# High and low rows side by side: matmuls of 256, 288 and 272 columns in place of three of 272

## The chip, the cores and the metric

The kernel runs on one core of a Trainium2 chip. The time is that of the device for one execution, in microseconds; lower is better.

## The reference

One decoder block on 256 tokens with 16 learned meta tokens ahead of them (272 rows in all), width 2048, all in float32. `hs` is the residual stream:

```
hs = concat([meta, x])                                     # (272, 2048)
hs = hs + 0.5 * swiglu(rmsnorm(hs, g1), gate1, up1, down1) # width 5632 inside
u  = rmsnorm(hs, gm) @ w_in + b_in                         # 5 groups of 1024: b, c, v, a, g
y_sc = b * causal_dwconv(c * v, 3 taps)
y_cf = silu(layernorm(causal_dwconv(a * sigmoid(g), 31 taps) + bias))
hs = hs + concat([y_sc, y_cf]) @ w_out
hs = hs + 0.5 * swiglu(rmsnorm(hs, g2), gate2, up2, down2)
out = rmsnorm(hs, gf)[16:]                                 # meta rows dropped
```

## The kernel before

The core holds everything transposed: 128 channels in the partitions, tokens along the free axis, so a tile of the residual stream is 128 x 272 and there are 16 of them (`res`). A weight block of 512 KB (`raw`) is fetched from HBM by SP, in a ring of 4. ScalarE rounds it to float32r as its high half (`high`, L726), VectorE subtracts and writes the low half (`low`, L955), TensorE takes both. Activations are kept as such halves as well: `x_hi` and `x_lo` (written by `operand`, ScalarE L734 and VectorE L964), and `a_hi` and `a_lo` for the hidden layer of the FFN (L777, L1039). `product` (L522 to L528) then does a tile of output as three matmuls into one PSUM bank: high weight with high activation, high weight with low, low weight with high. Each has its own weight load of 128 x 128.

The stages in order, with the groups of output columns, the blocks of a group and the columns of a matmul: gu1 (gate and up of the first FFN; 22 groups of 8 blocks, 272), down1 (4 of 22, 272), ag (4 of 8, 272), cv (4 of 8, 260: the 256 tokens and four meta tokens that the short convolution looks back on), b (2 of 8, 256), out_sc and out_cf (4 of 4 each, 256), gu2 (22 of 8, 256), down2 (4 of 22, 512, with tokens in the partitions). A block is 24 matmuls, in down2 12. A group of results fills 4 of the 8 PSUM banks, and the next group the other 4.

Each engine's program runs in its written order. VectorE empties a group's banks during the third block of the next group (`finish` at step 0, L1026 and L1028, times `rstd`), and the rest of the group's work stands at the next two blocks. ScalarE's share stands after its fourth to sixth weight block. In ag, cv, b and out_sc both engines also do the 31-tap convolution (`conv_products`, `conv_adds`), a fixed number of taps after each block (`spread`).

Addresses are chosen by hand, modulo 256 bytes. A row of `x_hi` or `a_hi` is 272 elements, 1088 bytes, so that the starts of successive rows move on by 64: 192, 0, 64, 128. gu1, down1, ag and b take the rows of a block from one such class (`down_rows`, `b_rows`, every fourth row) and write the weight block at the address 64 bytes past the class (`w_class`, `w_same`, `w_kept`). gu2 and the out stages have rows of 1024 bytes at class 192 and weights at class 0. cv takes rows in order, with weights at class 0 throughout.

Of the kernel before, what the change touches and what calls it, by code (L numbers as in the profile page):

```python
# [26 lines left out]
ALU = mybir.AluOpType  # L27
# [4 lines left out]
P = 128  # L32
# [7 lines left out]
def build(nc, x, meta_tokens, ffn1_norm, ffn1_w_gate, ffn1_w_up, ffn1_w_down, mix_norm, w_in, b_in,  # L40
# [40 lines left out]
    with ExitStack() as ctx:  # L81
# [9 lines left out]
        ROW_BLOCK, BUFFER = T, 4 * T  # L91
        sb("to_rows", [P, (192 - nc.sbuf_base) % 256 // 32 * 8])
# [4 lines left out]
        gain1 = sb("gain1", [P, KD])  # L97
# [3 lines left out]
        assert w_at % 256 == 0 and x_at % 256 == a_at % 256 == 192 and 4 * BUFFER % 256 == 0  # L101
# [21 lines left out]
        x_hi = at("x_hi", x_at, [P, KD, T], F32R)  # L123
        x_lo = at("x_lo", x_at + 4 * KD * T, [P, KD, T], F32R)
        x2_hi = at("x2_hi", x_at + 0, [P, KD, SEQ], F32R)
        x2_lo = at("x2_lo", x_at + 0 + 4 * KD * SEQ, [P, KD, SEQ], F32R)

        def weights(name, rows, pitch, shift):

            n = BLOCK // rows  # L130
            lead = shift(0) % 32 // 4
            both = [[at(f"{name}_{part}{s}", w_at + 4 * (BUFFER * (RING * b + s) - lead) + shift(s),
                        [P, rows, pitch], F32R)[:, :, lead:lead + n] for s in range(RING)]
                    for b, part in enumerate(("hi", "lo"))]
            assert all(shift(s) + 4 * ((rows - 1) * pitch + n) <= 4 * BUFFER for s in range(RING))
            return both

        NEAR = SEQ + -(-(SCW - 1) // 4) * 4
        w_rows = weights("w_rows", 4, ROW_BLOCK, lambda s: 0)
        w_class = [weights(f"w_class{q}_", 4, 256, lambda s: 256 // 4 * q) for q in range(4)]  # L140
        w_same = [weights(f"w_same{q}_", 2, BANK, lambda s: 256 // 4 * q) for q in range(4)]
        w_kept = [weights(f"w_kept{q}_", 2, BANK, lambda s: 256 // 4 * q + 4 * META) for q in range(4)]
        w_next = {q: weights(f"w_next{q}_", 2, BANK + META, lambda s: 256 // 4 * q) for q in (0, 2)}


        down_rows = []
        for q in (0, 2):
            up, down = list(range(q, KF, 4)), list(range(q + 1, KF, 4))[::-1]
            turn_at = up + down
            down_rows += [tuple(sorted(turn_at[t:t + 2])) for t in range(0, len(turn_at), 2)]  # L150
        assert sorted(k for pair in down_rows for k in pair) == list(range(KF))
        assert all(b - a in (1, 4) for a, b in down_rows)

        b_rows = [(k, k + 4) for q in range(4) for k in (q, q + 8)]
        assert len(b_rows) == N_B

        def block_weights(phase, g, i):

            s = slot(phase, g, i)
            if phase in ("gu1", "ag"):  # L160
                both = w_rows if isinstance(g, int) and g == 0 else w_class[i // 2]
            elif phase == "down1":
                a, b = down_rows[i]
                both = w_same[a % 4] if b == a + 4 else w_next[a % 4]
            elif phase == "b":
                both = w_kept[b_rows[i][0] % 4]
            else:
                both = w_class[0] if phase in ("cv", "gu2") else w_same[0]
            return both[0][s], both[1][s]

        def raw_rows(phase, s):
# [5 lines left out]
        a1_hi = at("a_hi", a_at, [P, KF, T], F32R)  # L177
        a1_lo = at("a_lo", a_at + 4 * KF * T, [P, KF, T], F32R)
        a2_both = at("a2_both", a_at + 64, [P, 2, KF, SEQ], F32R)
        a_of = {"gu1": (a1_hi, a1_lo),  # L180
                "gu2": (a2_both[:, 0, :, :], a2_both[:, 1, :, :])}
# [7 lines left out]
        mix_at = a_at + 0  # L189
# [28 lines left out]
        def param(name, i):  # L218
            if name == "ffn1":
                return gain1[:, i:i + 1]  # L220
            return par[:, 0, row0[name] + i:row0[name] + i + 1]

# [49 lines left out]
        ident_doubled = sem("ident_doubled")  # L272
        res_turned, res_copied, res_added = sem("res_turned"), sem("res_copied"), sem("res_added")
# [62 lines left out]


# [29 lines left out]
        def _(sp):  # L367
# [27 lines left out]
            def paired(phase, wa, wb, col_a, col_b):  # L395

                rows = [w.rearrange("(q c p) n -> q p c n", c=4, p=P) for w in (wa, wb)]
                every_fourth = [w.rearrange("(c q p) n -> q p c n", q=4, p=P) for w in (wa, wb)]

                def body(g, parity):  # L400
                    for i in range(n_blocks[phase]):
                        if phase == "gu1" and isinstance(g, int) and g == 0:
                            for q in {0: (0,), 2: (1,), 4: (2, 3)}.get(i, ()):
                                load_x(q)
                        apart = phase in ("gu1", "ag") and not (isinstance(g, int) and g == 0)
                        src = (every_fourth if apart else rows)[i % 2][
                            i // 2, :, :, bass.ds(g * 256 + (col_a, col_b)[i % 2], 256)]
# [70 lines left out]
        def _(pe):  # L478
# [43 lines left out]

            def product(bank, n, w_high, w_low, act_high, act_low, first, last):
# [26 lines left out]
            def paired(phase, norm):  # L550
                toks = tokens(phase)

                def body(g, parity):
# [6 lines left out]
                    for i in range(n_blocks[phase]):  # L560
# [8 lines left out]
                        for j, c in ([(j, c) for j in range(2) for c in range(4)] if phase in ("cv", "gu2")  # L569
                                     else [(j, c) for c in range(4) for j in range(2)]):  # L570
                                k = i // 2 + 4 * c if phase in ("gu1", "ag") and not first_group else 4 * (i // 2) + c
                                if norm and first_group and i % 2 == 0 and j == 0:
                                    pe.wait_ge(xlo_ready[norm], k + 1)
                                if opening and i == 0 and c == 2 and j == 0:
# [3 lines left out]
                                moving = ((x2_hi[:, k, :], x2_lo[:, k, :]) if phase == "gu2"  # L578
                                          else (x_hi[:, k, toks], x_lo[:, k, toks]))
                                m = product(bank, width[phase], w_hi[:, c, cols], w_lo[:, c, cols],  # L580
                                            *moving, k == 0, k == KD - 1)
# [7 lines left out]
            def pairs_group(phase, g, row_pairs, high, low):  # L589

                toks = tokens(phase)
                start_group(phase, g)
                for i, rows in enumerate(row_pairs):
                    start_block(phase, g, i)
                    if phase == "down1" and g == 0:
                        pe.wait_ge(alo_ready["gu1"], max(max(pair) for pair in down_rows[:i + 1]) // 2 + 1)
                    w_hi, w_lo = block_weights(phase, g, i)
                    for c, k in enumerate(rows):
                        for j in range(SET):
                            cols = slice(j * P, (j + 1) * P)  # L600
                            m = product(SET * (g % 2) + j, width[phase], w_hi[:, c, cols], w_lo[:, c, cols],
                                        high[:, k, toks], low[:, k, toks], i == 0 and c == 0,
                                        i == len(row_pairs) - 1 and c == 1)
# [22 lines left out]
            def last_group(g):  # L626
# [7 lines left out]
                def half_block(i, h):  # L634
# [3 lines left out]
                        for c in range(2):  # L638
                            k = 2 * i + c
                            w_high, w_low = (w[:, c, :] for w in block_weights("down2", g, i))  # L640
                            a_hi, a_lo = a_of["gu2"]
                            pe.matmul(dst, a_hi[:, k, toks], w_high, start=k == 0, stop=False)  # L642
                            pe.matmul(dst, a_lo[:, k, toks], w_high, start=False, stop=False)  # L643
                            m = pe.matmul(dst, a_hi[:, k, toks], w_low, start=False, stop=k == KF - 1)  # L644
# [53 lines left out]
            for g in range(G_D):  # L698
                pairs_group("down1", g, down_rows, a1_hi, a1_lo)
            paired("ag", "down1")  # L700
            paired("cv", None)
            for g in range(G_B):
                pairs_group("b", g, b_rows, x_hi, x_lo)
# [13 lines left out]
        def _(act):  # L717
# [10 lines left out]
            def operand(phase, norm, t):  # L728
# [4 lines left out]
                dst = x2_hi[:, t, :] if phase == "gu2" else x_hi[:, t, toks]  # L733
                act.activation(dst, res[:, t, toks], ACT.Copy,  # L734
# [619 lines left out]
```

## Time and profile before

| what | us |
|---|---|
| median of 3 runs | 1851.77 |
| lowest, highest of them | 1849.19, 1852.44 |
| span of the profiled execution (no other total is listed for it) | 1847.9 |
| TensorE, VectorE, ScalarE busy in that span | 1836.8, 1089.4, 902.2 |

The span reaches from the first to the last instruction of that execution. Matmuls are pipelined: a new one starts before the last has ended, so their busy time is not the sum of their durations, and their spacing has to be read from windows or starting times.

### The profile page before, as it was taken

The numbers are of one execution on the slowest core, as the hardware profiler recorded it, in microseconds if no ns is written. First come the engines' busy times: TensorE is split into PE (matmuls) and PEld (weight loads), VectorE is DVE, ScalarE is ACT, GpSimd is POOL, SyncE is SP. The second block draws the span as 40 slices with busy tenths as digits, with TensorE's granted clock in tenths as the row PEclk, the third lists the DMA queues.
The fourth block names the chain that finished last, engine by engine and source line by source line (L and its number), as shares of the span: only waits on it lengthen the run. The fifth ranks groups of instructions, "written<-read, shape, count | busy, mean of one in ns | idle before, by whom it ended". The sixth has DMA issues, their size and how long they took to land.

```text
span 1847.9 us, 34890 instructions
## 1 busy us (share of the span) xinstructions
PE 1836.8 (99%) x14421; PEld 1792.6 (97%) x14421; DVE 1089.4 (59%) x1230; ACT 902.2 (49%) x1151; POOL 5.8 (0%) x16
## 2 busy tenths in 40 slices
PE   9999999999999999999999999999999999999998
PEld 9999999999999999999999999999999999988886
DVE  7555555555554555369899887555555555544454
ACT  6434334344443444359888665444444444444443
POOL 1000000000000000000000000000000000000000
PEclk9999999999999999999999999999999999999999
DMA  7655555555567777755666566666666666666664
GB/s 229 193 177 178 174 181 174 178 178 174 181 172 180 177 177 179 179 175 175 185 184 180 176 209 192 194 194 192 193 192 194 192 194 192 215 193 189 193 189 135
DMA packets 283359, 342.29 MB, mean 185 GB/s; under 512 B 10639, under 2 KB 223985, under 8 KB 283152
## 3 DMA queue, kind: packets, MB, share of 16 engines
q1 hardware_dynamic: 282672, 340.44, 61.7%
q8 instruction: 59, 0.97, 0.2%
q10 hardware_dynamic: 320, 0.53, 0.1%
q0 software_dynamic: 288, 0.19, 0.0%
q14 instruction: 20, 0.16, 0.0%
HBM read 339.02 MB, written 2.10 MB: 185 GB/s over the span
## 4 chain that ended last, share of the span: by engine, by line
PE 97%; ACT 1%; DVE 1%; DMA 1%; issue 0%; SPq 0%; DVEq 0%
PE ps L526 28%; PE ps L528 28%; PE ps L527 28%; PE ps L642 4%; PE ps L643 4%; PE ps L644 4%; ACT tap_product L833 0%; DMA raw<-in_w_out 0%; DMA m_rows<-in_meta_tokens 0%; PE ps L660 0%; PE ps L488 0%; DVE w_same__lo L955 0%; ACT w_same__hi L726 0%; ACT y_f L850 0%; PE ps L667 0%
## 5 line engine op out<-in xcount | busy, mean ns | idle before, releaser
L528 PE MATMUL ps<-x_hi,w_class__lo 128*128 128x272 f32 (+2 forms) x3200 | 901.6, 282 | 0.0
L526 PE MATMUL ps<-x_hi,w_class__hi 128*128 128x272 f32 (+2 forms) x3200 | 900.8, 281 | 0.1
L527 PE MATMUL ps<-x_lo,w_class__hi 128*128 128x272 f32 (+2 forms) x3200 | 900.3, 281 | 0.0
L955 DVE TENSOR_TENSOR w_class__lo<-raw,w_class__hi 128x1024 fp32r<-128x1024 f32 x400 | 489.3, 1224 | 421.1 <-ACT w_class__hi L726 419.7
L726 ACT ACTIVATE w_class__hi<-raw 128x1024 fp32r<-128x1024 f32 x400 | 424.3, 1061 | 564.1 <-PE ps L528 563.8
L527 PEld LDWEIGHTS ps<-x_lo,w_class__hi 128*128 128x128 f32 x3200 | 602.3, 188 | 0.0
L526 PEld LDWEIGHTS ps<-x_hi,w_class__hi 128*128 128x128 f32 x3200 | 601.5, 188 | 0.3 <-PE ps L542 0.3
L528 PEld LDWEIGHTS ps<-x_hi,w_class__lo 128*128 128x128 f32 x3200 | 601.6, 188 | 0.0
L955 DVE TENSOR_TENSOR w_same__lo<-raw,w_same__hi 128x1024 fp32r<-128x1024 f32 x200 | 244.1, 1224 | 256.9 <-ACT w_same__hi L726 256.7
L726 ACT ACTIVATE w_same__hi<-raw 128x1024 fp32r<-128x1024 f32 x200 | 211.5, 1060 | 315.7 <-PE ps L528 170.6
L528 PE MATMUL ps<-a_hi,w_same__lo 128*128 128x272 f32 x640 | 183.4, 287 | 0.0
L526 PE MATMUL ps<-a_hi,w_same__hi 128*128 128x272 f32 x640 | 183.4, 287 | 0.0
L527 PE MATMUL ps<-a_lo,w_same__hi 128*128 128x272 f32 x640 | 183.3, 286 | 0.0
L642 PE MATMUL ps<-w_same__hi,a_both 128*128 128x512 f32 x352 | 137.3, 390 | 0.0
L644 PE MATMUL ps<-w_same__lo,a_both 128*128 128x512 f32 x352 | 137.0, 389 | 0.0
L643 PE MATMUL ps<-w_same__hi,a_both 128*128 128x512 f32 x352 | 137.0, 389 | 0.0
L527 PEld LDWEIGHTS ps<-a_lo,w_same__hi 128*128 128x128 f32 x640 | 120.6, 188 | 0.0
L526 PEld LDWEIGHTS ps<-a_hi,w_same__hi 128*128 128x128 f32 x640 | 120.5, 188 | 0.0
L528 PEld LDWEIGHTS ps<-a_hi,w_same__lo 128*128 128x128 f32 x640 | 120.5, 188 | 0.0
L833 ACT ACTIVATE tap_product<-z,par 128x256 f32<-128x256 f32 x232 | 98.8, 495 | 0.0
L644 PEld LDWEIGHTS ps<-w_same__lo,a_both 128*128 128x128 f32 x352 | 66.1, 188 | 13.8
L642 PEld LDWEIGHTS ps<-w_same__hi,a_both 128*128 128x128 f32 x352 | 66.1, 188 | 13.6
(170 smaller groups left out, 1509.5 us busy)
## 6 DMA issues: line engine op xcount, KB each, us to landing
raw<-in_ffn_w_up SPq DMA_DIRECT2D x176, 512.0 KB, 3.5
raw<-in_ffn_w_down SPq DMA_DIRECT2D x176, 512.0 KB, 4.9
raw<-in_ffn_w_gate SPq DMA_DIRECT2D x175, 512.0 KB, 3.5
raw<-in_w_in SPq DMA_DIRECT2D x80, 512.0 KB, 3.6
raw<-in_w_out SPq DMA_DIRECT2D x32, 512.0 KB, 4.8
x_tok<-in_x SPq DMA_DIRECT2D x4, 512.0 KB, 8.4
gain_tok<-in_final_norm SPq DMA_DIRECT2D x1, 1024.0 KB, 4.6
out_y<-o_tok SPq DMA_DIRECT2D x2, 512.0 KB, 2.8
```

The costliest lines, as they stand in the source:

```text
L526: pe.matmul(dst, w_high, act_high, start=first, stop=False)
L527: pe.matmul(dst, w_high, act_low, start=False, stop=False)
L528: return pe.matmul(dst, w_low, act_high, start=False, stop=last)
L642: pe.matmul(dst, a_hi[:, k, toks], w_high, start=k == 0, stop=False)
L643: pe.matmul(dst, a_lo[:, k, toks], w_high, start=False, stop=False)
L644: m = pe.matmul(dst, a_hi[:, k, toks], w_low, start=False, stop=k == KF - 1)
L726: act.activation(block_weights(phase, g, i)[0], raw_rows(phase, s), ACT.Copy).then_inc(hi_ready, 1)
L833: act.activation(tap_product[:, q % PRODUCTS, c % 2, :], z[:, c, 2 + n:2 + n + SEQ], ACT.Copy, scale=cf_tap(2 + n, c)).then_inc(cf_product, 1)
L955: dve.tensor_tensor(w_lo, raw_rows(phase, s), w_hi.bitcast(F32), ALU.subtract).then_inc(lo_ready, 1)
```

## The change

A row of moving data now holds one tile's high and low part side by side: high of the 256 tokens, high of the 16 meta tokens, low of the 16 meta tokens, low of the 256 tokens, 544 elements or 2176 bytes. Row starts are at 0 or 128 modulo 256 bytes. The middle of a row is read in one piece by the product of the high weight with the low part, which takes the high meta part along; the first matmul needs only the 256 tokens. The meta results come out in two pieces of the bank, which VectorE adds. In gu1, down1 and ag the three matmuls have 256, 288 and 272 columns, in cv 256, 276 and 272. b reads the same rows with three of 256. `in_rows` (`e` below) is 16, in cv 4; `in_order` is true in the first group of gu1 and ag alone; `add_meta_pieces` is one tensor_reduce from two pieces of 4 banks to 4 x e columns in SBUF.

```
+        HIGH_SEQ, HIGH_META = slice(0, SEQ), slice(SEQ, T)
+        LOW_META, LOW_SEQ = slice(T, T + META), slice(T + META, 2 * T)
...
+            def product_of_rows(phase, bank, w_high, w_low, row, first, last):
+                e = in_rows[phase]
+                seq = slice(e + META, e + META + SEQ)
+                pe.matmul(ps[:, bank, seq], w_high, row[:, HIGH_SEQ], start=first, stop=False, skip_group_check=True)
+                pe.matmul(ps[:, bank, 0:seq.stop], w_high, row[:, T - e:2 * T], start=False, stop=False,
+                          skip_group_check=True)
+                return pe.matmul(ps[:, bank, seq.start:seq.stop + META], w_low, row[:, 0:T], start=False, stop=last,
+                                 skip_group_check=True)
```

Weights and rows: there are two classes instead of four, 0 and 128, with the weights 64 bytes on; in the first group of gu1 and ag the weights stay at 64. cv takes every second row too.

```
+        w_class = [weights(f"w_class{q}_", 4, 256, 64 + 128 * q) for q in range(2)]
+        w_pair = [weights(f"w_pair{q}_", 2, BANK, 64 + 128 * q) for q in range(2)]
+        w_kept = [weights(f"w_kept{q}_", 2, BANK, 64 + 128 * q, 64 + 128 * (1 - q)) for q in range(2)]
+        def two_apart(n):
+            return [(k, k + 2) for first in range(0, n, 4) for k in (first, first + 1)]
+        down_rows, b_rows = two_apart(KF), two_apart(KD)
...
+            if in_order(phase, g):
+                return 4 * (i // 2) + c
+            q = i // 2
+            return 8 * (q // 2) + q % 2 + 2 * c
```

VectorE, in `finish` (gu1, ag, cv at step 0; down1 has the reduce and one addition into `res` instead):

```
+                        if phase in in_rows:
+                            add_meta_pieces(phase, bank)
...
+                            dve.tensor_tensor(piece, piece, over_two(rstd[:, toks.start:toks.start + e], e, SET),
+                                              ALU.mult).then_inc(meta_scaled[phase], 1)
+                            dve.wait_ge(meta_scaled[phase], g + 1)
+                            dve.wait_ge(emptied, read + 4)
+                            dve.tensor_tensor(t12[:, :, 0:e], t12[:, :, 0:e], piece,
+                                              ALU.add).then_inc(meta_whole[phase], 1)
```

ScalarE's SiLU, sigmoid and Identity at that place now wait for `meta_whole` instead of `emptied`. `operand` and the halves of `a` are written in two instructions each on ScalarE and VectorE, one for the tokens and one for the meta tokens:

```
-                dst = x2_hi[:, t, :] if phase == "gu2" else x_hi[:, t, toks]
-                act.activation(dst, res[:, t, toks], ACT.Copy,
+                    act.activation(x_rows[:, t, HIGH_SEQ], res[:, t, META:T], ACT.Copy,
...
+                    act.activation(x_rows[:, t, HIGH_META], res[:, t, 0:META], ACT.Copy,
```

gu2, out_sc, out_cf and down2 keep their lengths and their addresses modulo 256.

## Rows read from the trace of the kernel before

**Rows 1.** The page: the span, and busy time, share, instructions of each engine.
```profile
span 1847.9 us, 34890 instructions
...
PE 1836.8 (99%) x14421; PEld 1792.6 (97%) x14421; DVE 1089.4 (59%) x1230; ACT 902.2 (49%) x1151; POOL 5.8 (0%) x16
```

**Rows 2.** The page: the chain that ended last, shares of the span by engine.
```profile
PE 97%; ACT 1%; DVE 1%; DMA 1%; issue 0%; SPq 0%; DVEq 0%
```

**Rows 3.** Waits of TensorE, all: who waited for whom, us in total, times, longest.
```profile
PE ps L508 <- DVE ones L949: 1.1, 1, 1.1
PE ps L526 <- DVE x_lo L964: 1.1, 1, 1.1
PE ps L518 <- DMA m_rows<-in_meta_tokens: 0.7, 1, 0.7
PE ps L526 <- DVE w_same__lo L955: 0.2, 1, 0.2
```

**Rows 4.** Groups of instructions by shape: busy us, mean ns of one, idle before.
```profile
L528 PE MATMUL ps<-x_hi,w_class__lo 128*128 128x272 f32 x1536 | 440.8, 287 | 0.0
...
L526 PE MATMUL ps<-x_hi,w_class__hi 128*128 128x256 f32 x1408 | 388.7, 276 | 0.1
```

**Rows 5.** Windows, TensorE: from:to, length, busy (instructions), clock, DMA share, GB/s.
```profile
84.67:250.66 165.99, 165.99 (x1346) 1.00 0.58 177
600.37:795.83 195.46, 195.46 (x1586) 1.00 0.73 179
820.34:891.48 71.14, 71.14 (x578) 1.00 0.59 176
914.37:983.01 68.64, 68.64 (x578) 1.00 0.60 185
983.01:988.46 5.45, 5.45 (x50) 1.00 0.46 117
988.46:994.11 5.65, 5.65 (x50) 1.00 0.63 180
994.11:999.58 5.47, 5.47 (x50) 1.00 0.72 215
999.58:1005.23 5.65, 5.65 (x50) 1.00 0.80 242
...
1139.42:1596.38 456.96, 456.96 (x4035) 1.00 0.62 192
1599.10:1626.30 27.20, 27.20 (x121) 1.00 0.74 247
```

**Rows 6.** Timeline, small instructions of VectorE, then ScalarE: start, us, what.
```profile
30.16 0.37 DVE L1235 TENSOR_REDUCE step<-ident 128x16 f32<-128x128 f32 x1
...
30.93 0.23 DVE L1241 TENSOR_SCALAR step<-step,tok 128x16 f32<-128x16 f32 x1
...
4.59 0.18 ACT L865 ACTIVATE gain<-ps 128x16 f32<-128x16 f32 x1 [2.05 <-PE ps L513]
```

**Rows 7.** Windows, three groups of ag: VectorE, then ScalarE.
```profile
820.34:891.48 71.14, 64.54 (x84) 1.00 0.59 176
...
820.34:891.48 71.14, 66.94 (x127) 1.00 0.59 176
```

**Rows 8.** Timeline of the start: the first matmul, x_lo's third tile, its matmul.
```profile
9.42 0.36 PE L526 MATMUL ps<-x_hi,w_rows_hi 128*128 128x272 f32 x1 [1.06 <-DVE x_lo L964]
...
10.20 0.91 DVE L964 SCALAR_TENSOR_TENSOR x_lo<-res,gain,x_hi 128x272 fp32r<-128x272 f32 x2
...
10.99 0.29 PE L526 MATMUL ps<-x_hi,w_rows_hi 128*128 128x272 f32 x1
```

**Rows 9.** Timeline, ag's first group: the sum of squares split, and its matmul.
```profile
803.30 0.44 DVE L972 TENSOR_TENSOR sum_lo<-step,sum_hi 128x272 fp32r<-128x272 f32 x1
...
807.93 0.28 PE L542 MATMUL ps<-sum_lo,ones_r 128*128 128x272 f32 x1
```

More of the change, by code:

```diff
@@ L122, in build @@
         sum_lo = at("sum_lo", sq_at + 4 * T, [P, T], F32R)
[L123 to L128, printed above, removed]
-            n = BLOCK // rows
[L131 to L135, printed above, removed]
+        x_rows = at("x_rows", x_at, [P, KD, 2 * T], F32R)
@@ new lines, in build, with weights @@
+        x2_hi = at("x2_hi", x_at + 192, [P, KD, SEQ], F32R)
+        x2_lo = at("x2_lo", x_at + 192 + 4 * KD * SEQ, [P, KD, SEQ], F32R)
+        HIGH_SEQ, HIGH_META = slice(0, SEQ), slice(SEQ, T)
+        LOW_META, LOW_SEQ = slice(T, T + META), slice(T + META, 2 * T)
+        def weights(name, rows, pitch, shift, low_shift=None):
+            n = BLOCK // rows
+            both = [[at(f"{name}_{part}{s}", w_at + 4 * BUFFER * (RING * b + s) + by, [P, rows, pitch], F32R)[:, :, 0:n]
+                     for s in range(RING)]
+                    for b, part, by in ((0, "hi", shift), (1, "lo", shift if low_shift is None else low_shift))]
+            assert max(shift, low_shift or 0) + 4 * ((rows - 1) * pitch + n) <= 4 * BUFFER
@@ L146, in build @@
[L146 to L155, printed above, removed]
+        w_wide = weights("w_wide", 4, 256, 0)
@@ L272, in build @@
         ident_doubled = sem("ident_doubled")
+        meta_added, meta_scaled, meta_whole = ({n: sem(f"{what}_{n}") for n in ("gu1", "down1", "ag", "cv")}
+                                               for what in ("meta_added", "meta_scaled", "meta_whole"))
         res_turned, res_copied, res_added = sem("res_turned"), sem("res_copied"), sem("res_added")
@@ L333, in tokens, with wanted, meta_pieces @@
             return slice(T - width[phase], T)
+        in_rows = {"gu1": T - SEQ, "down1": T - SEQ, "ag": T - SEQ, "cv": NEAR - SEQ}
+        LAST_META = META + T
+        def wanted(phase):
+            return slice(META, META + width[phase]) if phase in in_rows else slice(0, width[phase])
+        def meta_pieces(phase, bank):
+            e = in_rows[phase]
+            return bass.AP(ps, bank * BANK, [[2 * SET * BANK, P], [BANK, SET], [1, e], [LAST_META, 2]])
         STEPS = CFW - 1
@@ L404, in body @@
                                 load_x(q)
-                        apart = phase in ("gu1", "ag") and not (isinstance(g, int) and g == 0)
-                        src = (every_fourth if apart else rows)[i % 2][
-                            i // 2, :, :, bass.ds(g * 256 + (col_a, col_b)[i % 2], 256)]
+                        cols = bass.ds(g * 256 + (col_a, col_b)[i % 2], 256)
+                        src = (rows[i % 2][i // 2, :, :, cols] if in_order(phase, g)
+                               else every_second[i % 2][i // 2 // 2, i // 2 % 2, :, :, cols])
                         if phase == "gu1" and isinstance(g, int) and g == 0 and i == 0:
@@ L577, in body @@
                                 bank = SET * parity + 2 * (i % 2) + j
[L578 to L581, printed above, removed]
+                                first, last = i < 2 and c == 0, i >= n_blocks[phase] - 2 and c == 3
+                                if phase == "gu2":
+                                    m = product(bank, SEQ, w_hi[:, c, cols], w_lo[:, c, cols],
+                                                x2_hi[:, k, :], x2_lo[:, k, :], first, last)
+                                else:
+                                    m = product_of_rows(phase, bank, w_hi[:, c, cols], w_lo[:, c, cols],
+                                                        x_rows[:, k, :], first, last)
                         m.then_inc(block_used, 1)
@@ L772, in finish @@
                     if at_step == 0:
-                        act.wait_ge(emptied, read + 2)
+                        if phase == "gu1":
+                            act.wait_ge(meta_whole[phase], g + 1)
+                        else:
+                            act.wait_ge(emptied, read + 2)
                         act.activation(t1[:, :, 0:w], t1[:, :, 0:w], ACT.Silu).then_inc(silu_ready[phase], 1)
```

177 lines of the change are left out of this document (114 added, 63 removed).

## The prediction

> **What bounds the kernel now.** I read the page's busy table first: TensorE is busy 99% of the span, VectorE 59%, ScalarE 49% [rows 1]. Then the chain that ended last: 97% of it is TensorE, nearly all on the three lines of `product` [rows 2]. Then TensorE's waits: the whole list sums to about 3 us [rows 3]. So the time is the number of matmuls times their spacing, and nothing else is long. The instruction durations don't give the spacing, since matmuls overlap: 287 ns is shown for one of 272 columns [rows 4], yet a new one starts every 123 ns. I take the spacing from windows that begin and end where a group of output columns begins. Their x counts include the one to three matmuls in flight at an edge, so I divide by the code's count (192 per group of gu1, ag and cv, 528 per group of down1). From rows 5, in their order:
>
> - gu1, 7 groups: 165.99/1344 = 123.51 ns for 272 columns; down1, 3 groups: 195.46/1584 = 123.40; ag, 3 groups: 71.14/576 = 123.51
> - cv, 3 groups, 260 columns: 68.64/576 = 119.17
> - b, 256 columns, four stretches of 48: 113.5, 117.7, 114.0, 117.7
> - gu2, 256 columns, 21 groups: 456.96/4032 = 113.33; down2, 512 columns: 27.20/120 = 226.67
>
> The granted clock is 1.00 in all of them, the 2.4 GHz level. 256 and 512 columns lie on one line through zero, 0.4427 ns a column. On that line 272 columns would take 120.4 and 260 columns 115.1. They take 3.0 and 4.1 more. That excess over the line is what the change can win: it leaves the columns of a product at 3 x 272 = 816 = 256 + 288 + 272, and makes one operand of the three a 256.
>
> **The change, part by part.**
>
> *Three products of 256, 288, 272.* It holds for gu1 (22 groups x 64 = 1408 products), down1 (704) and ag (256), 2368 in all. Before, one takes 3 x 123.51 = 370.5 ns in gu1 and ag, 3 x 123.40 = 370.2 in down1 [rows 5]. After: the 256 at gu2's 113.3 and the 272 at 123.4. 288 columns are in no row. From below it is the line, 127.5. From above it is the line plus the largest excess seen, the 4.3 ns by which b's slow stretches exceed gu2: 131.8. I take 130.4, the excess of the nearest length, 272. The sum is 113.3 + 130.4 + 123.4 = 367.1 ns. That saves 3.4 x 1664 + 3.1 x 704 = 7.9 us. If all three lay on the line (361.2) it would be 21.6 us; if the 256 ran at b's 117.7 and the 288 at 131.8, the product would be 372.9, 5.9 us more than now.
>
> *Where operands start.* A row of moving data starts at one of two places modulo 256 bytes (0 or 128) instead of four, and the weight one chunk of 64 bytes further, as now. b shows that such places matter: its rows start at 0, 64, 128, 192, in that order, and 0 and 128 are the fast ones [rows 5]. After, only 0 and 128 are left there. That saves 0.20 + 0.18 us in each of its two groups, 0.8 us (bounds 0 and 0.8). The Trainium skill, "SBUF — State Buffer", section "SBUF: two separate sides", says that PE, ACT and VectorE's own pair "never wait on anyone", and the table there gives TensorE a second, independent read port for weights. By that rule places would cost nothing and b would save nothing. b's 113.5 against 117.7 at equal length speaks against its completeness.
>
> *Changes of place.* gu1 changes place four times in 192 matmuls, down1 four times in 528. From 123.51 and 123.40 [rows 5] a change costs t with 4t/192 - 4t/528 = 0.11 ns, so 8.2 ns. down1 now takes row pairs two apart, a change at each of 22 blocks: 18 more x 4 groups x 8.2 ns = 0.6 us; b has 4 more in each group, 0.1 us. Bounds: 0, and twice that if the longer jump costs twice. In the first group of gu1 and of ag the weights stay at one place while rows alternate: 0.2 us, with cv's excess of 4.1 in place of 3.0 on their 384 matmuls as upper bound (0.4).
>
> *cv.* Its products grow from 780 to 256 + 276 + 272 = 804 columns, and the 276 start 48 bytes past a place, as cv's operands do now. Before 357.5 ns, after 113.3 + (122.2 + 4.1) + 123.4 = 363.0 [rows 5]: 256 products x 5.5 ns = 1.4 us more (at least 0.4, if the 276 lay on the line).
>
> *VectorE's and ScalarE's added work.* Each group of gu1, ag and cv gets a reduce out of PSUM, a product with rstd and an addition; down1 gets a reduce and an addition; operands and halves of `a` are written in two pieces, the second of 16 columns per tile. The nearest rows are a 128x128 to 128x16 reduce, 0.37 us, a 16 column tensor_scalar, 0.23, and a 16 column ScalarE copy, 0.18 [rows 6]. So VectorE gets 0.37 + 2 x 0.23 = 0.8 us a group, in gu1 0.2 more for the low part of `a`, of 23.7. The tightest place is ag with its convolution steps: VectorE is busy 64.54 of 71.14 us there, ScalarE 66.94 [rows 7], so per group 2.2 and 1.4 us are idle. The sigmoid of ag now waits for the whole meta columns, 0.8 us later; behind it on ScalarE stand the convolution products and the next weight high half, and VectorE's low half and TensorE behind that. It fits into 1.4, and the four weight buffers give three blocks of 2.96 us as lead. Cost zero; without that cover 0.8 us x 8 groups of ag and cv = 6.4.
>
> *The start.* The first matmul waits for x_lo [rows 8]. Each tile now costs VectorE a second instruction of some 0.2 us. x_lo of the third and fourth tile is written from 10.20 to 11.11, the third by about 10.7, and TensorE reaches the third at 10.99 [rows 8]: with three small instructions ahead it is late by 0.3; 0.2 more at the first matmul, and the second block's low half is behind them too. I take 0.6 us, bounds 0 and 1.5. At down1's end the sum of squares is split by 803.74 and read at 807.9 [rows 9]: 4 us of slack hide about 2 us of added small instructions.
>
> *The end of the convolution.* out_sc is where TensorE waits for a low half at all [rows 3]; ScalarE and VectorE reach it with a little more behind them: 0.4 us, bounds 0 and 2.
>
> *gu2, out_sc, out_cf, down2* keep lengths and places: zero. The results now stand at columns 16 to 287 of a PSUM bank instead of 0 to 271; VectorE's reads of them keep their size, and I count nothing.
>
> Sum: -7.9 - 0.8 + 0.1 + 0.6 + 0.2 + 1.4 + 0.6 + 0.4 = -5.4 us. It is made against the profiled span, 1847.9, which would become 1842.5. The page gives no total for that execution beyond its span; the median of the three runs is 1851.8, 3.9 above the span, and I subtract from the median: **1846.4 us**.
>
> **Rivals.**
>
> A. *Only the columns count.* Then 816 columns cost what they cost now, the excess merely moves (to the 288, or to the boundaries between unequal lengths), and the additions are left: -5.4 + 7.9 = +2.5, 1854.3 us. For it: every stage of the trace runs one length at a time, so none shows what a mix does. Against it: 272 columns take 10.1 ns more than 256, not the 7.1 of the line, and 512 no excess. The Trainium skill, "TensorE: Matmul & The Clock Gate", section "Back-to-back issue gap", gives a warm gap of N / 2.4 + 2.5 ns, a fixed cost per matmul whatever N: an estimate by it is 109.2 and 115.8 ns for 256 and 272, and no change for a product. The measured 113.3 and 123.5 don't follow it, so I give this case no more than its share below.
>
> B. *288 columns lie on the line*, being an even number of 64-byte chunks, as 256 and 512 are: 3.0 x 2368 = 7.0 us better (2.9 unrounded) than the forecast, 1839.4. For it: the lengths without excess are the even ones. Against: cv's and b's excess don't come from parity alone.
>
> C. *Slower: the 256 never settle.* Mixed with unequal lengths, the 256 run at b's slow 117.7 and the 288 at 131.8, b doesn't gain (+0.8). Product 372.9, +5.9 in place of -7.9: +9.2 us, 1861.0. It decides where the three together exceed 370.5 less the 1 ns or so that the additions are worth per product. For it: b's slow stretches are 256 columns at the same clock and matched places. Against: gu2 and the out stages are steady at 113.3.
>
> D. *ScalarE in ag falls behind.* The idle 1.4 us a group is used up and TensorE waits for the low halves, 0.8 us in each of 8 groups: +6.4, 1852.8. Against: the lead of three blocks.
>
> **Chances.** Forecast 0.40, A 0.20, B 0.18, C 0.12, D 0.10. Less than 0.2% (3.7 us) can't be told from no change here. Faster by more than that: 0.36 of the forecast's 0.40 and B, 0.02 of D: 0.56. Within: 0.04 + 0.16 + 0.08 = 0.28. Slower: 0.04 of A and C: 0.16. The range goes from B, 1839, to between A and C, 1857; C and all on the line (some 1832.7) stay outside.
>
> **What would show it.** In windows of whole groups: gu1 below 23.71 us a group (23.5 by the forecast, 23.7 by A, 23.3 by B, 23.9 by C); within a product, starts after the 256, 288 and 272 of 113, 130 and 123 ns; cv 23.2 instead of 22.88; b's four stretches all near 5.46; VectorE busy some 38 us more (22 groups by 1.0, 4 by 0.6, 8 by 0.8, 32 operands by 0.23), TensorE's waits still a few us. The forecast is wrong if the 256 take over 116 ns or the 288 over 133, or if TensorE waits for low halves in ag.

## The result, and the profile after

The changed kernel takes 1865.57 us (median of 4 runs, 1864.26 to 1866.04) against 1850.77 for the one before (1849.19 to 1852.44). The ratio is 1.008, its 95% interval 1.0066 to 1.0094: slower by 0.8%, where 0.3% faster was forecast and 1839 to 1857 was the range. The profiled executions differ by the same amount, 1862.5 against 1847.9. Beside the later runs the kernel before took 1849.2 to 1853.6 us in 38 of its 41 executions and 1870.4 to 1870.7 in three, and k5 below took some 20 us more in two of its six; the ratios of k3, k4 and k5 and their intervals count these in, so the ratio of the medians stands beside them.

The page of the changed kernel (the span; busy time, share and instructions) says that the kind of bound has not changed:

```profile
span 1862.5 us, 35140 instructions
...
PE 1851.0 (99%) x14421; PEld 1806.5 (97%) x14421; DVE 1112.4 (60%) x1382; ACT 912.3 (49%) x1205; POOL 5.8 (0%) x16
```

TensorE does as many matmuls as in [rows 1] and is busy 14.2 us longer, nearly the whole difference. Its waits in the changed kernel (who waited for whom, us in total, times, longest) are as short as in [rows 3]; these are the four longest of six, the other two are of 0.2 us each:

```profile
PE ps L551 <- DVE x_rows L1027: 1.2, 1, 1.2
PE ps L532 <- DVE ones L1004: 1.1, 1, 1.1
PE ps L575 <- DVE sum_lo L1035: 0.6, 1, 0.6
PE ps L560 <- DVE w_plain_lo L1010: 0.2, 1, 0.2
```

So the loss is in the spacing. Windows of TensorE in the changed kernel answer to [rows 5] (from:to, length, busy and count, clock, transfers); they are, in their order, seven groups of gu1, the last two of down1, three of ag, three of cv, the first of b, three of out_cf, 21 of gu2:

```profile
86.08:253.43 167.35, 167.35 (x1347) 1.00 0.55 175
671.87:803.43 131.56, 131.56 (x1059) 1.00 0.53 177
828.00:899.72 71.72, 71.72 (x579) 1.00 0.56 173
923.37:994.28 70.91, 70.91 (x578) 1.00 0.58 179
994.28:1017.30 23.02, 23.02 (x195) 1.00 0.62 184
1097.15:1131.07 33.92, 33.92 (x290) 1.00 0.67 213
1153.84:1610.80 456.96, 456.96 (x4034) 1.00 0.62 192
```

By the code's counts (1344, 1056, 576, 576, 192, 288, 4032) that is 124.5, 124.6, 124.5, 123.1, 119.9, 117.8 and 113.33 ns a matmul, against 123.5, 123.4, 123.5, 119.2, a mean of 115.7 for b, 113.3 for out_cf and 113.33. A product of gu1 went from 370.5 to 373.5 ns. Within it, by starting times over a group, 118.1 ns pass from the start of the 256 to the next start, 132.0 from that of the 288 and 123.4 from that of the 272. The streams of TensorE alone with the same product (below) mostly split it alike, but two of seven take 116.3, 129.2 and 127.9 with the same sum.

Where the 14.6 us went, by the starts of the stages in both traces:

| stage | before, us | after, us | difference |
|---|---|---|---|
| up to gu1's first product | 9.4 | 9.3 | -0.2 |
| gu1, first group | 27.8 | 29.0 | +1.2 |
| gu1, the other 21 | 498.0 | 502.0 | +4.1 |
| down1 | 260.6 | 263.1 | +2.5 |
| ag | 95.7 | 96.3 | +0.6 |
| cv | 91.5 | 94.6 | +3.0 |
| b | 44.7 | 46.2 | +1.6 |
| out_sc, out_cf | 89.4 | 90.5 | +1.1 |
| gu2 | 479.3 | 479.7 | +0.4 |
| down2 and the end | 251.5 | 251.7 | +0.2 |

### The profile page after: what moved, and what is told of

It reads as the page before. It is cut to its first block, busy times and chain, and to the rows that moved or that the text cites. A ratio compares the mean times of both kernels' runs of the same rounds, so it can differ in the third digit from the quotient of the medians.

```text
span 1862.5 us, 35140 instructions
## 1 busy us (share of the span) xinstructions
PE 1851.0 (99%) x14421; PEld 1806.5 (97%) x14421; DVE 1112.4 (60%) x1382; ACT 912.3 (49%) x1205; POOL 5.8 (0%) x16
## 4 chain that ended last, share of the span: by engine, by line
PE 97%; ACT 1%; DVE 1%; issue 0%; DMA 0%; DVEq 0%; ACTq 0%
PE ps L552 18%; PE ps L554 17%; PE ps L551 16%; PE ps L560 11%; PE ps L562 11%; PE ps L561 11%; PE ps L682 4%; PE ps L681 4%; PE ps L683 4%; ACT tap_product L888 0%; ACT x_rows L776 0%; DMA gain_rows<-in_ffn_norm 0%; DVE res L1308 0%; ACT w_class__hi L765 0%; PE ps L699 0%
## 5 line engine op out<-in xcount | busy, mean ns | idle before, releaser
L552 PE MATMUL ps<-x_rows,w_class__hi 128*128 128x288 f32 (+1 forms) x1920 | 565.8, 295 | 0.0
L554 PE MATMUL ps<-x_rows,w_class__lo 128*128 128x272 f32 x1920 | 551.5, 287 | 0.0
L551 PE MATMUL ps<-x_rows,w_class__hi 128*128 128x256 f32 x1920 | 540.3, 281 | 1.3 <-DVE x_rows L1027 1.2
L560 PE MATMUL ps<-x_hi,w_wide_hi 128*128 128x256 f32 x1408 | 389.2, 276 | 0.1
L561 PE MATMUL ps<-x_lo,w_wide_hi 128*128 128x256 f32 x1408 | 389.1, 276 | 0.0
L562 PE MATMUL ps<-x_hi,w_wide_lo 128*128 128x256 f32 x1408 | 389.1, 276 | 0.0
L551 PEld LDWEIGHTS ps<-x_rows,w_class__hi 128*128 128x128 f32 x1920 | 362.9, 189 | 2.1 <-DVE w_class__lo L1317 1.4
L554 PEld LDWEIGHTS ps<-x_rows,w_class__lo 128*128 128x128 f32 x1920 | 361.1, 188 | 0.0
L552 PEld LDWEIGHTS ps<-x_rows,w_class__hi 128*128 128x128 f32 x1920 | 360.7, 188 | 0.0
L560 PEld LDWEIGHTS ps<-x_hi,w_wide_hi 128*128 128x128 f32 x1408 | 264.4, 188 | 0.3 <-PE ps L576 0.3
L562 PEld LDWEIGHTS ps<-x_hi,w_wide_lo 128*128 128x128 f32 x1408 | 264.5, 188 | 0.0
L1010 DVE TENSOR_TENSOR w_plain_lo<-raw,w_plain_hi 128x1024 fp32r<-128x1024 f32 x120 | 146.2, 1224 | 132.3 <-ACT w_plain_hi L765 132.2
L765 ACT ACTIVATE w_plain_hi<-raw 128x1024 fp32r<-128x1024 f32 x120 | 126.7, 1059 | 170.0 <-PE ps L683 132.3
```

Source lines behind the costliest of these rows:

```text
L551: pe.matmul(ps[:, bank, seq], w_high, row[:, HIGH_SEQ], start=first, stop=False, skip_group_check=True)
L552: pe.matmul(ps[:, bank, 0:seq.stop], w_high, row[:, T - e:2 * T], start=False, stop=False, skip_group_check=True)
L554: return pe.matmul(ps[:, bank, seq.start:seq.stop + META], w_low, row[:, 0:T], start=False, stop=last, skip_group_check=True)
L560: pe.matmul(dst, w_high, act_high, start=first, stop=False)
L561: pe.matmul(dst, w_high, act_low, start=False, stop=False)
L562: return pe.matmul(dst, w_low, act_high, start=False, stop=last)
```

## The experiments

Most of the questions can be asked of TensorE alone. For that there is a kernel without any of the block: it fills two areas of SBUF from x, and issues streams of matmuls, each matmul with its own load of 128 weight columns, in the pattern of gu1's blocks, a wait for the end of the stream before ahead of each (a drain, below). The code cuts are shortened. "Place" below means an address modulo 256 bytes. Of its windows the first 24 matmuls of a stream are cut off; 167 spacings are left where nothing else is said, whatever the x count says.

### One stream per question, TensorE alone (micro1)

```
+ # gu1 before                        + # gu1 after
+ matmul(.., w_hi, M[r: r+272])       + matmul(ps[.., 32:288], w_hi, M[r: r+256])
+ matmul(.., w_hi, M[r+lo: +272])     + matmul(ps[.., 0:288],  w_hi, M[r+256: r+544])
+ matmul(.., w_lo, M[r: r+272])       + matmul(ps[.., 32:304], w_lo, M[r: r+272])
```

> TensorE alone: no weight preparation, no transfers, 32 streams of 192 matmuls each behind a drain (the last one without), x as data; out is a copy of x, the rest of the block is left out. Streams repeat the addresses of gu2 (3 x 256), gu1 before (3 x 272), gu1 after (256, 288, 272), b after, cv before, then change one thing: PSUM columns, order, lengths, the place of the weights. Theory (mixed lengths leave the 256 in the slow spacing of about 118 ns): gu2's stream 113.3 ns, gu1 before 123.3, gu1 after 118 + 132 + 123.5 = 373.5 ns a product, also with PSUM from column 0; the new rows with 3 x 272 go back to 370. Rival 1 (the new rows and places, not the lengths): 3 x 272 in the new rows stay above 372. Rival 2 (PSUM columns 16 to 303): from column 0 the product falls to 370 or less. Rival 3 (ScalarE, VectorE or transfers press on TensorE's reads): alone, all streams fall to the line, 0.443 ns a column, 361 for the product.

Windows of TensorE in that kernel: gu2's stream, gu1 before, gu1 after, the same with PSUM from column 0, b after, 3 x 192, 3 x 240, cv before:

```profile
29.39:48.31 18.92, 18.92 (x169) 1.00 0.01 2
51.71:72.31 20.60, 20.60 (x169) 1.00 0.00 1
75.74:96.52 20.78, 20.78 (x169) 1.00 0.01 2
99.96:120.74 20.78, 20.78 (x169) 1.00 0.00 1
172.52:192.71 20.19, 20.19 (x170) 1.00 0.01 2
341.93:360.58 18.65, 18.65 (x170) 1.00 0.00 1
363.71:382.41 18.70, 18.70 (x170) 1.00 0.01 2
757.54:777.36 19.82, 19.82 (x170) 1.00 0.00 1
```

113.3, 123.35, 124.4, 124.4, 120.9, 111.7, 112.0 and 118.7 ns. The numbers of gu1 and gu2 come out with the other engines idle and the transfer share at 0.01: in these stages they press on nothing, and the PSUM columns don't matter. b (119.9 in the kernel) and cv (119.2) come out less closely. 3 x 272 read from the new rows took 124.46, which looked like the rows; but there the low row starts at place 64 and the weights don't move with it. The streams of 192 and 240 columns are near a floor: 64 columns less than 256 win only 1.7 ns. The weight load that each matmul brings may be the reason; no stream without it was run.

### Three matmuls of 272 in the changed kernel (k1_all272)

```
-  pe.matmul(ps[:, bank, seq], w_high, row[:, HIGH_SEQ], ...)
-  pe.matmul(ps[:, bank, 0:seq.stop], w_high, row[:, T - e:2 * T], ...)
+  pe.matmul(ps[:, bank, seq.start:seq.stop + META], w_high, row[:, 0:T], ...)
+  pe.matmul(ps[:, bank, seq.start - e:seq.stop], w_high, row[:, 2 * T - SEQ - e:2 * T], ...)
```

> The changed kernel with its rows, places, order of blocks and additions, but three matmuls of 272 columns (in cv 272, 260, 272). Theory of the lengths: a product of gu1, down1 and ag goes from 373.5 back to about 370.4 ns, 3.1 x 2368 = 7.3 us, so about 1858 us against 1865.6. Rival, the new rows and places: gu1 stays at 23.91 us a group, about 1865.

1861.53 us, ratio to the kernel before 1.0062 (1.0046 to 1.0079). Eight groups of gu1:

```profile
62.48:253.52 191.04, 191.04 (x1538) 1.00 0.58 176
```

191.04/8 = 23.88 us a group, hardly less than 23.91. The experiment did not separate the two theories: it also moved the middle operand 64 bytes off its place, as the stream above. (A line that the cut leaves out lets the reduce read one piece of each bank instead of two.) Its span is 2.8 us shorter than the changed kernel's: 1.2 of it in gu1 and down1, 0.7 in cv (93.9 us against 94.6), the rest mostly in out_cf, which ran at 113.3 here.

### VectorE's additions left out (k2_no_adds)

```
-  add_meta_pieces(phase, bank)
-  dve.tensor_tensor(piece, piece, over_two(rstd[...], e, SET), ALU.mult)
-  dve.tensor_tensor(t12[:, :, 0:e], t12[:, :, 0:e], piece, ALU.add)
```

> The changed kernel without VectorE's reduce, product and additions on the meta pieces (the meta rows' partial sums are left out) and without the waits for them. If these are hidden, as predicted, 0 to -0.5 us against the changed kernel, 1865; if VectorE or ScalarE bounds ag, up to 6 us less, 1859, and TensorE's waits in the trace of the changed kernel would go.

1864.62 us against 1865.57 of the changed kernel; ratio to the kernel before 1.0078 (1.0062 to 1.0095). Eight groups of gu1:

```profile
62.71:253.96 191.25, 191.25 (x1538) 1.00 0.57 176
```

They stay at 23.91 us (191.25/8). Its span is 0.9 us shorter, and out_cf and the start of gu2, at 113.3 in this execution, give more than that. The additions are hidden. The operands written in two pieces are still there, so this run doesn't test them.

### Lengths and rows apart, and other places (micro2)

```
+ # lengths only: M rows of 272, low part 17408 bytes on, all at place 0, weights at 64
+ matmul 256 from r ; 288 from r + lo ; 272 from r
+ # rows only: new rows, all at place 0, weights at 64
+ matmul 272 from r ; 272 from r + 1024 bytes ; 272 from r
```

> TensorE alone again (the block is left out, out is a copy of x), streams of 192 matmuls behind a drain each. Streams 2 and 3 change only the lengths at the old addresses, stream 4 only the rows (3 x 272 read from the new rows, every operand at its place). Theory of the lengths: 2 and 3 at 124.4 ns mean, 4 at 123.3. Rival, the rows: 2 and 3 at 123.3, 4 at 124.4. Then the changed product with 15 other places of the high and low weights: if the places chosen are the best, all are above 124.4; if a better pair exists, it falls below 123.3. Four matmuls of 272 whose operands move on by 64 bytes each: if what costs is that a matmul of 17 chunks of 64 bytes breaks the round of four, 120.4; if not, 123.3. One matmul of 272 inside a stream of 256: if the slow spacing of 256 columns is a state that a stream keeps, it is 113.3 before and 117.8 after; if not, 113.3 after it too. The last three streams run without a drain between them: 113.3, 120, then 117.8 by the same theory.

gu1 before, lengths only (at gu1's own addresses), rows only, gu1 after, then the changed product with the weights at 0 (high) and 64 (low), and at 192 and 128:

```profile
30.57:51.17 20.60, 20.60 (x170) 1.00 0.01 2
54.60:75.38 20.78, 20.78 (x169) 1.00 0.00 1
103.02:123.62 20.60, 20.60 (x169) 1.00 0.00 1
127.06:147.84 20.78, 20.78 (x169) 1.00 0.01 2
175.64:196.79 21.15, 21.15 (x170) 1.00 0.01 2
468.21:488.81 20.60, 20.60 (x170) 1.00 0.01 2
```

Lengths alone: 124.4. Rows alone: 123.35. That settles the first question. Over 16 pairs of places the changed product takes 123.35 to 126.67 ns a matmul; the best only reaches the old one. Three matmuls became four of 272 whose starts move on by 64 bytes each: 126.1 ns, not the 120.4 of that idea.

One long matmul in a stream of 256: 70 spacings before and 70 behind a single 272 (first two rows), then a single 320 (last two):

```profile
1077.07:1085.01 7.94, 7.94 (x73) 1.00 0.01 2
1088.10:1096.03 7.93, 7.93 (x72) 1.00 0.01 2
1099.21:1107.15 7.94, 7.94 (x73) 1.00 0.00 0
1110.34:1118.59 8.25, 8.25 (x73) 1.00 0.00 0
```

113.4 before and 113.3 after the 272 (its own spacing is 121 ns, the five behind it 117 to 123), but 113.4 before and 117.8 behind the 320, to the end of the stream. At the same addresses 256 columns have two steady spacings. The last three streams, 3 x 256 behind a drain, then without one with the weights at 0 and at 64:

```profile
1121.86:1141.52 19.66, 19.66 (x169) 1.00 0.01 2
1144.52:1164.56 20.04, 20.04 (x170) 1.00 0.00 1
1167.50:1187.17 19.67, 19.67 (x169) 1.00 0.01 2
```

117.7, 120.0 and 117.8: the first was expected at 113.3, so a drain in front does not ensure the fast spacing.

### The best pair of places in the changed kernel (k3_places)

```
-  w_class = [weights(.., 64 + 128 * q) ..]       # and w_pair
+  w_class = [weights(.., 192 - 128 * q, 128 - 128 * q) ..]
```

> The changed kernel with its 256, 288 and 272 columns; only the places of the weight halves in gu1, down1, ag and cv move: high 192 bytes past the row's place, low 128, in place of 64 for both. Alone on TensorE that pair took 123.35 ns a matmul, the pair of the changed kernel 124.45. Theory (what costs is how the reads of the next weights fall against the reads of the running matmul): gu1 23.7 us a group in place of 23.91, 3.3 ns x 2368 products = 7.8 us less than the changed kernel, 1857.7. Rival (in the kernel the writes of the two other engines or the change of place between blocks set it): no change, 1865.

1861.21 us, ratio 1.0038 (1.0006 to 1.0069), of the medians 1.0060. Eight groups of gu1, then down1:

```profile
62.38:252.57 190.19, 190.19 (x1538) 1.00 0.56 177
537.85:800.38 262.53, 262.53 (x2114) 1.00 0.53 177
```

gu1 takes 190.19/8 = 23.77 us a group (123.8 ns a matmul), down1 124.3 ns. The places matter in the kernel too, but of 7.8 us the span gained 2.9. Changes of place account for what is missing in these two stages: over the 123.35 of the stream, gu1 (4 changes in 192 matmuls) and down1 (22 in 528) lose 23 ns a change alike. That is an estimate from these figures; in micro4 below, the stream with these places moving took 123.65 ns, which is 17 ns a change.

### Three of 272, every operand at its place (k4_272_at_places)

```
+  pe.matmul(ps[:, bank, seq.start:seq.stop + META], w_high, row[:, 0:T], ...)
+  pe.matmul(ps[:, bank, 0:SEQ + e], w_high, row[:, SEQ:2 * SEQ + e], ...)
```

> The changed kernel with three matmuls of 272 columns from the new rows (in cv 272, 260, 272), the middle one from byte 1024 of the row, where the 288 started, so that every operand stays at its place; it reads the wrong columns for the low part (last 16 low tokens left out, meta in double), so values are not the block's. Theory of the lengths: gu1 back to 23.7 us a group, 7.8 us less than the changed kernel, 1857.7. Rival, the rows or the added work: 23.9.

1857.42 us, ratio 1.0026 (1.0002 to 1.0049), of the medians 1.0039. Eight groups of gu1, then b's first group:

```profile
62.18:251.83 189.65, 189.65 (x1538) 1.00 0.56 177
987.74:1010.75 23.01, 23.01 (x194) 1.00 0.60 182
```

189.65/8 = 23.71 us, the figure of the kernel before, with the new rows, the two places and all the added work in it. The span is 8.5 us under the changed kernel's; some 1.9 of that is out_cf and the start of gu2, which ran at 113.3 in this execution. So the three lengths cost 0.20 us a group of gu1 by themselves, and b, untouched here, keeps its loss. cv keeps its loss too (94.7 us) though it has 272, 260 and 272 columns here.

### 108 arrangements (micro3)

> TensorE alone (the block is left out, out is a copy of x), 108 streams of 96 matmuls: 3 x 272 with the low row at four places and high and low weights at four each (64 streams), 3 x 256 with the low row 128 on and 16 pairs of weights' places (b after), 3 x 260 at 16 pairs and at three odd starts with four places (cv). If the place of the old kernel is the best that there is, none of the first 64 is under 370.0 ns a product; a pair below would be a faster kernel. For b: a pair at 113.3 in place of 120.9. For 260 columns: something under the 119.2 of cv before.

3 x 272 with the high weights at the row's place and the low 64 on; the old arrangement; then 3 x 256 with the low row 128 on and b's new weights moved from 192 to 128, and as they were (72 spacings each):

```profile
42.64:51.44 8.80, 8.80 (x75) 1.00 0.01 2
91.78:100.66 8.88, 8.88 (x75) 1.00 0.01 2
890.79:899.12 8.33, 8.33 (x75) 1.00 0.00 0
902.31:911.02 8.71, 8.71 (x74) 1.00 0.00 0
```

122.2, 123.3, 115.7 and 121.0 ns. Of the 64 for 272 columns one is below the old kernel's 123.3 and one more equals it; the rest go up to 126.7. For 260 columns 118.4 was the lowest, against cv's 119.2.

### That arrangement in the kernel before (k5_before_high0)

```
-  w_class = [weights(.., lambda s: 256 // 4 * q) for q in range(4)]     # low and high; also w_same, w_next
+  w_class = [weights(.., lambda s: 256 // 4 * q, lambda s: (192 + 64 * q) % 256) for q in range(4)]   # low, high
```

> The kernel before, with its three matmuls of 272 columns and its rows; in gu1 (all groups but the first), ag (the same) and down1 the high half of the weights lies at the row's own place modulo 256 bytes, the low half stays 64 bytes on. Alone on TensorE that was the best of 64 arrangements: 122.21 ns a matmul against 123.35. If the places of the weights against the rows set the spacing in the kernel too, a group of gu1 takes 23.49 us in place of 23.71, 23 x 0.22 + 4 x 0.6 + ... = 2304 products x 3.4 ns = 7.8 us less than before, 1842. Rival (each change of place throws the stream into a worse spacing, as in the changed kernel with moved places, which won 2.9 of 7.8 us): between 1847 and 1852.

1871.99 us, ratio 1.016 (1.012 to 1.020), of the medians 1.012: slower than both kernels. gu1's groups took 24.30 us:

```profile
61.88:256.28 194.40, 194.40 (x1538) 1.00 0.56 173
```

That is 126.6 ns a matmul, in gu1, down1 and ag together 21 us more than before. What a stream showed once was not the spacing that the kernel gets.

### The same stream again and again (micro4)

> TensorE alone (the block is left out, out is a copy of x), 29 streams of 192 matmuls. The arrangement that alone took 122.2 ns took 126.6 in the kernel. Theory (a stream has several steady spacings at the same addresses, and what came before picks one): with the place moving on every 48 matmuls, as in the kernel, it falls to about 126.6 without any other engine; drained at each move it is 122.2 apart from the drains; right behind another stream, without a drain, it isn't 122.2. 256 columns behind eight drains: 113.3 in some, 117.8 in others. Rival (the other engines or the start at 192): moving places leave it at 122.2, or the one place with rows at 192 is at 126.6 by itself. For the changed kernel: one place 124.45, moving 124.5; with the moved weights 123.35 at one place, 123.8 when it moves; before: 123.33 and 123.5.

High at 0 and low at 64, rows at 0: the third stream of the kernel and the first of its four repeats; then one stream of 3 x 256, the same code four times in a row, behind a drain each:

```profile
77.19:97.60 20.41, 20.41 (x169) 1.00 0.01 2
525.33:546.48 21.15, 21.15 (x169) 1.00 0.00 1
344.94:364.61 19.67, 19.67 (x169) 1.00 0.00 1
367.80:386.73 18.93, 18.93 (x170) 1.00 0.01 2
389.99:409.66 19.67, 19.67 (x170) 1.00 0.00 1
412.85:431.77 18.92, 18.92 (x169) 1.00 0.01 2
```

122.2 once (as in micro3) and 126.7 four times; 117.8, 113.3, 117.8, 113.3, and so on through all eight. The old product gave 123.33 or 123.34 in each of its six streams at one place and 123.47 with the place moving, the changed one 124.46 and 124.51. Moving places put the "best" arrangement at 126.0, so no other engine is needed. A drain at each move doesn't bring it back (132.3 with the drains' own cost in it), against my theory that it would. With rows at 192 by themselves it was 124.5 behind a drain and 126.7 right behind another stream: that part is open.

### b's weights moved (k6_kept)

```
-  w_kept = [weights(.., 64 + 128 * q, 64 + 128 * (1 - q)) for q in range(2)]
+  w_kept = [weights(.., 64 + 128 * q, 128 - 128 * q) for q in range(2)]
```

> The changed kernel with one edit in b: the low half of the weights 128 bytes on (row class 0; 0 for class 128) in place of 192. Alone on TensorE, behind a drain, 3 x 256 with the low row 128 on took 120.9 ns with b's places after the change and 115.6 with these. If the distance of weights and rows sets b's spacing, b's two groups (23.02 and 23.23 us) fall to about 22.2 and 22.4, 1.6 us in all; if a change of place at each block keeps the stream from its good spacing, they stay above 22.8.

One execution, 1863.98 us. b's two groups:

```profile
995.10:1017.31 22.21, 22.21 (x194) 1.00 0.64 182
1017.31:1039.74 22.43, 22.38 (x194) 1.00 0.60 195
```

The two groups take 22.21 and 22.43 us against 23.02 and 23.23, as expected, and as in the kernel before ([rows 5] gives 22.22 for the first): b's loss was the place of its low weights against rows whose low part starts 128 bytes on. The whole execution was only 0.3 us shorter than the changed kernel's (span 1862.2 against 1862.5): gu1 began 0.8 us later and out_sc took 0.5 us more. With one execution, b's gain is shown and a gain of the whole is not.

## Why the prediction was wrong

**What bounds the kernel** held: TensorE's spacing, waits of 3 us, everything else hidden.

**Three products of 256, 288, 272: the step that failed.** I added up spacings of single lengths: gu2's 113.3 for the 256, taken from a stage in which every matmul has 256 columns, with b's 117.7 as an upper bound. In the kernel's mix the 256 take 118.1, over the 116 that I had named as a sign of being wrong. The 288 took 132.0, just above my end of 131.8; the 272 were right at 123.4. Together 373.5 ns in place of 367.1, so +3.0 where -3.4 stood. Over 2368 products (my 5.9 us of C against measured 7.2, from 4.1 + 2.5 + 0.6 in the table) this is +7.2 where -7.9 was forecast, 15 of the 20 us between the -5.4 of my sum and the +14.6 of the traces. micro2 and k4 show that the lengths do it alone. So the rival C was the case: its mechanism (256 near b's slow spacing), its product (372.9) and its time (1861.0) are close, and it got 0.12. What should have raised that chance stood in [rows 5]: b has 256 columns at the same clock in stretches of 113.5 and 117.7, so a spacing of 256 columns was not a constant, and I explained the stretches by the start of the row alone. That reading had a counterexample: b's fourth stretch has its rows at 192 and its weights at 0, as gu2 has, and took 117.7 where gu2 took 113.3. Since micro4's eight equal streams alternate between 117.8 and 113.3 too, b's stretches may be the two spacings in turn and owe nothing to the start; no run tells the two apart. The sum is firmer than the split: the seven streams of this product whose weights stay 64 bytes past the rows all take 373.3 to 373.6 ns, five of them split 118, 132 and 123 as the kernel does, two 116, 129 and 128.

**Where operands start.** I expected b to gain 0.8 us since its rows now start at 0 and 128. It lost 1.6. Instead of alternating, its stretches all run at 119.8 to 120.0. The high and low parts of a row now start 128 bytes apart, and in the old kernel at one place; the diff said so, and I priced only the row. k6 gives these 1.6 us of b back. By the Trainium skill, "SBUF — State Buffer", section "SBUF: two separate sides", PE never waits on anyone, and a table there gives it a second, independent read port for weights. micro1 agrees on the neighbours as far as it goes: idle or busy, they leave the spacing of gu1 and gu2 alike (123.35 and 123.5, 113.3 and 113.3). But moving only b's low weights against its rows changes its groups by 3.5% (k6), which a separate port for weights would not lead one to expect.

**cv.** +1.4 forecast, +3.0 measured: its 256 at 117.0, its 276 at 127.4, its 272 at 125.0 ns by starting times, not 113.3, 126.3 and 123.4. Single-length figures failed here too, but the cause is open: k4 has 272, 260 and 272 columns in cv, the same 804, and takes 94.7 us as well, so making the first one longer wins nothing, and cv's weights moved from 0 to 64 bytes on in both.

**Changes of place** (0.6 forecast) can't be told from the lengths in down1 of the changed kernel. In k4 down1 takes 123.61 ns against 123.40 before, 0.21 x 2112 = 0.4 us. The price depends on the places: in k3 it is some 23 ns a change, not 8.2.

**Added work.** Hidden outside the start, as predicted: k2 for the additions, TensorE's list of waits for the operands written in two pieces. VectorE is busy 23.0 us more, not 38: the reduce took 0.29 us, the two small instructions 0.22 each, and consecutive instructions overlap. ScalarE in ag didn't fall behind (D): it is busy 66.70 of 71.72 us in the three groups of [rows 7], and TensorE waits for nothing there.

**The start**: +1.2 for gu1's first group and -0.2 ahead of it, 0.6 forecast. The cause was elsewhere than I put it. VectorE finishes the split sum of squares late, and TensorE stands (timeline, VectorE and then TensorE):

```profile
34.11 0.44 DVE L1035 TENSOR_TENSOR sum_lo<-step,sum_hi 128x272 fp32r<-128x272 f32 x1
...
34.60 0.39 PE L575 MATMUL ps<-sum_hi,ones_r 128*128 128x272 f32 x1 [0.63 <-DVE sum_lo L1035]
```

It ended at 32.4 before; 16 tiles with a second small instruction of 0.23 us are ahead of it. By starting times a tile takes 0.54 us where it took 0.42, which makes 2.0 of the 2.2 us.

**gu2 and out_cf: zero** was wrong by 1.9 us (out_sc, where I had 0.4 more, took 0.3 less). out_cf ran at 117.8 ns in the profiled execution, as did the first blocks of gu2 up to their wait at 1142, with unchanged lengths and places. It ran at 113.3 in k1, k2 and k4 and at 117.8 in k3 and k6, whose out stages are the same code. These are the two spacings of micro4, and part of the profiled difference therefore need not be the change's own. What picks one I can't say. It may also be what parts the executions of one kernel: out_cf and gu2's first group differ by 1.9 us between the two, and k4's ten executions fall into four of 1855.7 to 1856.2 (the profiled one, at 113.3, among them) and six of 1857.4 to 1858.8. By an estimate, all 4608 matmuls of out_cf and gu2 at 117.78 in place of 113.33 make 20.5 us, the step of the three executions of the kernel before at 1870. No trace of such an execution was taken, so this is not shown.

**A** is out (a product is 3 ns longer, not equal), and with it, for these float32r streams, the fixed 2.5 ns per matmul of the Trainium skill, "TensorE: Matmul & The Clock Gate", section "Back-to-back issue gap": an estimate by it gives both products the same time. The page gives the figure for an isolated matmul and says itself that streams with weight loads depart from it. **B** is out too: 3 x 288 took 131.7 to 133.35 ns a matmul alone, by the place of the weights, against 127.5 on the line, and 3 x 320, also an even number of 64-byte chunks, 146.7, 5.0 above the line.

Nothing run here beats the kernel before. To the account of the changed kernel: k4 and k6 together would come to some 1856 if b's gain held for the whole, still above it, with cv (3.1 us), the start (1.2) and 0.5 in down1 as what is left; they weren't run together.

## What to carry to other kernels

The spacing of back-to-back matmuls belongs to the stream, not to the matmul: a figure read in a stage of one length does not hold in a mix, so a trade of columns between matmuls has to be timed in its mix. A stream of TensorE alone reproduced the spacing to 0.2 ns in gu1 and gu2, 0.5 in cv before and 1.0 in b after, but run it several times and with the kernel's own steps of address: a spacing seen once may be one of two. A stage whose equal instructions show two spacings in the profile says that no single figure of it may be used as a price.

## What the runs showed of the hardware

- At the same addresses and with the same code, 256-column matmuls ran at 113.33 or 117.78 ns, eight streams in strict turn; one 320-column matmul in the middle switched the rest of a stream, one of 272 didn't. Of the 206 streams of three matmuls a product, 115 ended at 340.0, 353.3, 360.0, 366.7, 370.0, 373.3 or 380.0 ns a product, all multiples of 3.33 ns (their last 16 products, by starting times).
- The place of a weight block modulo 256 bytes against the running operand's is worth up to 6.7 ns a matmul: 3 x 256 took 113.3 (or 117.8, as above) with weights 64 bytes on, 120.0 at 0, and in one stream each 118.7 at 128 and 117.8 at 192, which can't be told from the second spacing; 3 x 512 took 226.7 at 0 and 233.3 at 64. Which distance is best depends on the length.
- Under 256 columns little is won: 192 and 240 columns took 111.7 and 112.0 ns against 113.3, with a weight load each.
- The split of a mixed product is less fixed than its sum: the changed product, with the same code, took 116.2, 129.2 and 128.0 ns in micro1 and 118.3, 131.7 and 123.4 in micro2, 373.3 or 373.4 together.
